# Order of waits, loads and vector work at five places of a hybrid decoder layer

## The reference

```
y_a = y_a @ w_proj_attn[layer]
y_b = o_d.reshape(b, s, D_VAL_B).astype(x.dtype) @ w_proj_delta[layer]
h = h + (gate_a * y_a + gate_b * y_b) @ w_out[layer]
hn = rmsnorm(h, norm_ffn[layer])
h = h + (jax.nn.silu(hn @ w_gate[layer]) * (hn @ w_up[layer])) @ w_down[layer]
return rmsnorm(h, norm_final)
```

## Time and profile before

| what | us |
|---|---|
| median of three runs | 2248.0 (2246.32 to 2248.94) |
| the profiled execution | 2246.41 |
| its span | 2244.7 |
| TensorE busy in it | 2187.7 |
| VectorE busy | 1119.6 |
| ScalarE busy | 917.5 |
| POOL busy | 698.9 |

### The profile page before, as it was taken

The page is one execution under the profiler, slowest core; times in us unless marked ns, Lnnn a source line. Parts: engine busy times, 40 slices in busy tenths (PEclk is TensorE's granted clock), DMA queues, the critical chain, the costliest instruction groups (busy, mean ns, idle before and its releaser), DMA issues.

```text
span 2244.7 us, 30780 instructions
## 1 busy us (share of the span) xinstructions
PE 2187.7 (97%) x11040; PEld 1823.9 (81%) x11040; DVE 1119.6 (50%) x1559; ACT 917.5 (41%) x1627; POOL 698.9 (31%) x529
## 2 busy tenths in 40 slices
PE   6999999999999999999999999999999999999998
PEld 4788787887878888888888887888788888878887
DVE  7621423314256656655665544425766666640054
ACT  5544444443345555555555632124433333320013
POOL 6885665666521111111111124321000000043340
PEclk8999999999999999999999999999999999999999
DMA  5112213123231211211211343341222222261221
GB/s 134 49 48 67 86 57 94 58 57 95 81 102 36 66 37 47 65 45 39 75 56 31 129 160 123 89 108 29 85 78 81 84 79 80 75 232 49 72 79 75
DMA packets 251922, 175.66 MB, mean 78 GB/s; under 512 B 41448, under 2 KB 225960, under 8 KB 251840
## 3 DMA queue, kind: packets, MB, share of 16 engines
q1 hardware_dynamic: 221776, 136.46, 20.7%
q10 hardware_dynamic: 30064, 38.10, 5.3%
HBM read 143.36 MB, written 31.18 MB: 78 GB/s over the span
## 4 chain that ended last, share of the span: by engine, by line
PE 85%; DVE 3%; ACT 3%; issue 3%; POOL 2%; DMA 2%; POOLq 1%; ACTq 1%; DVEq 1%; SPq 0%
PE bank L213 19%; PE bank L2273 16%; PE bank L1064 15%; PE bank L2514 10%; PE bank L1277 6%; PE bank L1527 2%; PE bank L1510 2%; PE bank L687 1%; PE bank L2289 1%; DMA raw_first<-in_w_in 1%; PE bank L1517 1%; PE bank L698 1%; PE bank L1564 1%; DVE own_sum_t L486 1%; POOL q_lo_s L941 1%
## 5 line engine op out<-in xcount | busy, mean ns | idle before, releaser
L213 PE MATMUL bank<-u_hi,w_hi 128*128 128x512 f32 x704 | 310.9, 442 | 4.2 <-ACT z_next L1749 3.0
L199 POOL CAST w_hi<-raw 128x1024 fp32r<-128x1024 f32 (+1 forms) x60 | 61.0, 1017 | 711.4 <-PE bank L213 484.7
L213 PE MATMUL bank<-u_hi,w_lo 128*128 128x512 f32 x704 | 277.0, 394 | 0.0
L213 PE MATMUL bank<-u_lo,w_hi 128*128 128x512 f32 x704 | 276.3, 392 | 0.0
L2495 POOL CAST dn_hi<-dn_raw 128x896 fp32r<-128x896 f32 (+1 forms) x24 | 31.2, 1301 | 564.9 <-DMA dn_raw<-in_w_down 460.5
L213 PEld LDWEIGHTS bank<-u_hi,w_lo 128*128 128x128 f32 x704 | 132.4, 188 | 29.0
L201 POOL TENSOR_TENSOR w_lo<-raw,w_hi 128x1024 fp32r<-128x1024 f32 (+1 forms) x60 | 151.2, 2520 | 8.6
L213 PEld LDWEIGHTS bank<-u_hi,w_hi 128*128 128x128 f32 x704 | 133.8, 190 | 20.3 <-ACT z_next L1749 3.4
L213 PEld LDWEIGHTS bank<-u_lo,w_hi 128*128 128x128 f32 x704 | 134.0, 190 | 15.0 <-issue 1.9
L941 POOL TENSOR_TENSOR q_lo_s<-q_sum_s,q_hi_s 128x512 fp32r<-128x512 f32 x92 | 122.1, 1333 | 72.8 <-ACT q_hi_s L996 67.2
L1817 DVE SCALAR_TENSOR_TENSOR conv_out<-conv_in,conv_c,conv_out 128x1024 f32<-128x1024 f32 (+1 forms) x96 | 100.3, 1045 | 15.0 <-issue 12.0
(11 more groups left out here) (433 smaller groups left out, 5864.5 us busy)
## 6 DMA issues: line engine op xcount, KB each, us to landing
raw<-in_w_in SPq DMA_DIRECT2D x36, 512.0 KB, 3.8
raw_first<-in_w_in SPq DMA_DIRECT2D x24, 512.0 KB, 3.7
raw_second<-in_w_in SPq DMA_DIRECT2D x24, 512.0 KB, 4.8
row<-scr_rows ACTq DMA_DIRECT2D x24, 512.0 KB, 4.7
raw_gate<-in_w_gate SPq DMA_DIRECT2D x22, 512.0 KB, 3.8
raw_up<-in_w_up SPq DMA_DIRECT2D x22, 512.0 KB, 3.8
scr_v<-gate_out SPq DMA_DIRECT2D x44, 256.0 KB, 2.1
tmp<-scr_gate ACTq DMA_DIRECT2D x16, 512.0 KB, 3.5
```

Of the source, the lines that this page charges most:

```text
L199: nc.gpsimd.tensor_copy(hi[:, 0:kt, :], raw[slot][:, 0:kt, :])
L213: last = nc.tensor.matmul(bank[dst][:, :], wpart[slot][wp][:, k, :], rhs[ap][:, k, half * HALF:(half + 1) * HALF], start=k == 0 and (wp, a ...
```

## The change

Five edits. In `proj_sp` the five branch loads (and the wait ahead of them) come after the load of the fifth weight tile instead of the fourth. In `merge_pe` the first group waits before each step k for the branches up to that step, in the order in which they are made, instead of for all twelve before the first. In `out_pe` the first tile runs its seven steps, the last step and the residual for both halves before the second tile begins; before, the seven steps of both tiles came first. In `up_vec` the step of a pair is divided into its additions (`up_add_vec`) and its work for the next pair (`up_next_vec`), and in the second pair of all the addition of step 4 comes ahead of the sums of step 3. In the last pair each subtraction of v comes one step later, so the first is behind the addition of step 4, and the fourth moves into `down_vec`.

```diff
@@ proj_sp
-                if f == 3:
+                if f == 4:
                     sp.wait_ge(dl["out"], NHB)
                     for t in range(NSLOT + 2, NB - 1):
                         load_branch(sp, t)
@@ merge_pe
                         if f == 0 and half == 0:
-                            pe.wait_ge(b_low, NB)
+                            pe.wait_ge(b_low, max(B_PLACE[NSLOT + kk] for kk in range(k + 1)) + 1)
@@ out_pe
                         product(0, i, half, k, (m_prod, 4 * KT - 3 + 2 * i + half))
-            pe.wait_ge(m_low, KT)
-            for i in range(2):
+                pe.wait_ge(m_low, KT)
                 for half in range(2):
                     product(0, i, half, KT - 1, None)
                     residual(0, i, half)
@@ up_step_vec, up_vec
+            up_add_vec(dve, it, b, i)
+            if not last:
+                up_next_vec(dve, it, b, i)
...
         def up_vec(dve):
-            for i in range(3, 7):
+            up_add_vec(dve, 0, 1, 4)
+            up_next_vec(dve, 0, 1, 3)
+            up_next_vec(dve, 0, 1, 4)
+            for i in range(5, 7):
                 up_step_vec(dve, 0, 1, i)
...
                     up_step_vec(dve, NFF // 2 - 1, b, i, last=b == 1)
-                    if b == 1 and i >= 3:
-                        v_low(dve, i - 3)
+                    if b == 1 and i >= 4:
+                        v_low(dve, i - 4)
@@ down_vec
-            for o in range(4, 7):
+            for o in range(3, 7):
                 v_low(dve, o)
```

More of the change, by code:

```diff
@@ L2323, in up_step_vec, with up_add_vec @@
         def up_step_vec(dve, it, b, i, last=False):
+            up_add_vec(dve, it, b, i)
+            if not last:
+                up_next_vec(dve, it, b, i)
+        def up_add_vec(dve, it, b, i):
             v = nc.vector
             p7, p3, p2 = it * 14 + 7 * b, it * 6 + 3 * b, it * 4 + 2 * b
-            q = it * 2 + (b + 1)
             first_bank, second_bank = bank[UP_BANKS[b][0]], bank[UP_BANKS[b][1]]
@@ L2349, in up_step_vec, with up_next_vec @@
                                     ALU.mult).then_inc(up["v"], 1)
-            if last:
-                return
+        def up_next_vec(dve, it, b, i):
+            q = it * 2 + (b + 1)
             if i == 2:
```

## The result

The changed kernel takes 2236.66 us (median of 5 runs, 2235.0 to 2238.16), the kernel before 2248.0: a ratio of 0.9949, 95% interval 0.9938 to 0.9960, so 11.3 us faster. Forecast were 6.7 us, to 2241.3, with a range down to 2238.0. The direction was right, the size too small, and the time lies outside the range. The profiled execution took 2236.66 us with a span of 2234.9, against 2246.41 and 2244.7: the two profiles differ by only 9.8 us. Both gaps, 6.7 to 9.8 and 9.8 to 11.3, had to be explained.

The account below looks back on a forecast made before the run. TensorE was taken as the bound, busy 2187.7 of 2244.7 us. Terms 0.57 + 2.56 + 1.19 + 1.2 + 2.9 = 8.4, less 1.7 for the clock, gave 6.7 us: 2241.3 from the median, range 2238.0 to 2245.0.

Parts of the forecast that it names:

- Weight ahead of branches: Attention projection: loading the fifth weight before the branch loads removes TensorE's wait, 0.57 us; possible loss 0 to 1.5 us.
- The 0.16 us that I added to each short idle: TensorE's short idles: first matmuls after resuming were taken as slower, costing 0.16 us beyond each idle.
- 3.13 and 3.37 in the table: Projection to first output matmul, two edits together: 3.13 us gain forecast, 3.37 us measured.
- Merge waits: Merge start: waiting branch by branch lets TensorE start without the 2.40 us idle; gain 2.56 us.
- idles near 3 us cost 1.7 us more, shorter ones do not: TensorE's idles: only those near 3 us bring the 1.2 GHz clock level behind them, losing 1.7 us.
- Output order: Output projection: closing the first tile early lets POOL start the next weight sooner; TensorE's wait goes, gain 1.19 us.
- First pair: Up projection: early addition starts TensorE 2.81 us sooner, but a new gate-half wait takes back 1.6; gain 1.2 us.
- Last pair: Up into down projection: TensorE 4.7 us early, then waits for the fourth down weight; gain 2.9, less 1.7 for the clock.
- chain of turns of VectorE and POOL: Down weights: the two engines' operations run one after the other, 10.5 us in sum, readying the fourth weight at 2004.4.
- my 90 matmuls: Down projection start: 90 matmuls, 20.4 us, have their data before TensorE needs the fourth down weight at 2000.8.
- the 1.7 us that I subtracted in vain: Down projection: the clock falls behind one 3.6 us idle, costing 1.70 us.
- The rival without slow matmuls: Down projection: no clock fall behind the new idle; gain 8.4 us, to 2239.6 us; chance 15%.

Follow-up runs that it names:

- e12: Kernel before with only the fifth projection weight loaded ahead of the five branch loads; 2247.17 us in one run.
- e2: Kernel before with only the merge's waits made branch by branch; 2244.01 us, ratio 0.9982.
- e1: Kernel before with only the last pair's edit, the addition of step 4 ahead of the first subtraction of v; 2243.43 us, ratio 0.998.
- e9: Kernel before, unedited, profiled again; 2247.95 us.
- e10: Kernel before, unedited, profiled once more; 2248.09 us.
- e11: Kernel before, unedited, third more profile; 2247.01 us.
- e8: Changed kernel with the next up weight's load issued ahead of the stores of the previous result; 2235.15 us, ratio 0.9945.
- e7: Changed kernel with the sixth and seventh subtraction of v (first chunk) replaced by ScalarE copies; 2238.32 us in one run.
- e6: Changed kernel, but the first down group waits for the third and fourth weight together before six matmuls; 2239.59 us, ratio 0.9967.
- e4: Kernel before with only the output projection's order changed, first tile ending first; 2247.86 us, ratio 0.9999.

## Why the prediction was right in direction and wrong in size

**Weight ahead of branches: right.** 0.57 us forecast, 0.7 in e12. The 0.16 us that I added to each short idle was misread, though: 2.79 is 2.40 plus a row's own 0.39 us, so 0.16 is by how much a row is longer than the distance to the next. Slower first matmuls come on top of it: behind the 0.41 us idle the distances are 0.34 us and four times 0.24, behind the 2.40 us idle one of 0.30. That makes up the 0.24 us between 3.13 and 3.37 in the table. The cover was thinner than I said, at a place that I did not look at: the sixth weight now lands behind the branches, POOL ends its split at 1343.01 + 1.29 = 1344.30, and TensorE needs it when the fifth tile, begun near 1339.0, has had its 24 matmuls, near 1344.4.

**Merge waits: mechanism right, the term too small.** The 2.56 us of the idle came (no idle in e2 and after; TensorE is at 1361.49 as the last subtraction runs). But the step "idles near 3 us cost 1.7 us more, shorter ones do not" was false. It rested on one profile. Of the eight profiles that have the 2.40 us idle, four (e1, e9, e10, e11) have the fall behind it. Of the kernel before alone it is three of four. So by my estimate about half of the executions, or more, paid 1.6 us more there, and the edit takes that away too: 0.8 us in the mean at one half, 1.2 at three quarters. The first pair's idle (1.77 to 2.70 us) had it in one of eight, 0.2 us more.

**Output order: right.** 1.19 forecast, 1.32 and 1.35 in the timelines; alone it is below what the medians can tell.

**First pair: right, with its new wait.** 1.2 forecast, 1.31 and 1.4 measured. VectorE's queue was the bound as worked out, and e8 shows what stood behind it: the transfer of the up weight, not VectorE's amount of work.

**Last pair: this step failed.** Forecast was a chain of turns of VectorE and POOL that ends at 2004.4, one idle of 3.6 us, and the 1.70 us of the low clock behind it, 1.2 us net. Measured 3.69 (e1: 3.75). The turns are real (e7), but two things were wrong. First, their end: in the frame of before it is 1997.61 + 6.03 = 2003.6, 0.8 us earlier than summed. Second, and larger, the form of the idle. I had TensorE pass the third weight and wait only for the fourth. POOL's subtraction for the third, 3.96 us beside VectorE, also came too late, by 0.88 us, and six matmuls stand between the two waits. My own chain said as much, had I asked it: its turns end the third weight at 1993.9 + 2.25 + 0.93 + 2.25 + 2.1 = 2001.4, and TensorE needs it six matmuls ahead of 2000.8, at 1999.4. The last six of my 90 matmuls did not have what they need. The idle was cut in two short ones, and the clock did not fall. e6 joins them and pays; e7 takes the first away and pays at 2.40 us. This is the 1.7 us that I subtracted in vain. The turns bind with little to spare: in the profile of after POOL begins the fourth weight at 1994.40, right behind the third with no idle, but in e7, where the turns are gone, it idles 1.82 us for that weight's transfer. The rival without slow matmuls, given 15%, was the case, and 2239.6 with it was still 3 us too high.

**The sum.** 3.37 + 1.32 + 1.31 + 3.69 = 9.7 is the difference of the two profiles. I carried the forecast from the profile's time to the median, 1.6 us higher, as if the edits could not touch that difference. They do: the profiled execution of before was one of those without the fall at the merge. Over the four profiles of before the way from the projection to the final sum is 916.81, 918.38, 917.40 and 917.77 us, mean 917.6; over the two of after 907.11 and 906.50, mean 906.8. That is 10.8 us, near the 11.3 of the medians and within their interval (9.0 to 13.9). The last half us stays open; it is below what these runs tell.

## What to carry to other kernels

An idle of TensorE above 2 us is to be priced with the low clock behind it, by its chance over several profiles, not by the one at hand; the first profile of this kernel hid a cost that four of eight profiles pay. Where an edit makes TensorE early at a bound that stays, the new idle's form matters as much as its length: two waits of 0.9 and 1.4 us with six matmuls between them were cheaper than one of 2.4. And when an engine is late by its queue, look at which transfer its first late operation waited for: moving the addition brought 1.3 of 2.8 us, and the rest came only with the load (e8).

## What the runs showed of the hardware

By idles before, and falls of the clock behind them (a stretch of 0.50 to 0.69 with matmuls of 0.63 us instead of 0.39), over the profiles that have them:

| idle of TensorE | us | with a fall |
|---|---|---|
| all others from the projection up to the final norm (many) | 0.4 to 1.77 | none |
| start of the DeltaNet phase, all profiles | 2.95 to 3.00 | 13 of 14 |
| a second idle there, e10 alone | 2.38 | 1 of 1 |
| start of the merge | 2.40 | 4 of 8 |
| last product of the first edited pair, in before and e1, e4, e9 to e12 | 2.13 to 2.70 | 1 of 7 |
| last product of the last pair | 2.23 to 3.05 | 7 of 8 |
| down weights, in one piece (e6, e7, e12) | 2.40, 2.91, 4.16 | 3 of 3 |

The shortest of these idles with a fall was 2.23 us and the longest without one 2.96, both in e10. In the final norm, where TensorE has little left to do, the clock also fell in after and e12, about 2 us behind an idle of 1.08, and no time was lost by it (10.7 us from there to the end, as in every profile). The same 2.40 us at the same instruction fell in four executions and not in four others, so length alone does not decide between these two; what does stays open. The fall did not come at one fixed moment either: from the projection on, the low level began between 0.7 us ahead of the resumption (e12, at the down weights) and 1.5 us behind it (e2, in the last pair). The price was 1.6 us at the merge, 1.7 at the last product, and more in e12.

VectorE's subtractions and POOL's operations run in turns: beside VectorE 3.96 us, without 2.13 (e7), for the same POOL subtraction. The rows of after show the turns one by one: VectorE's subtraction ends at 1992.49, 2.15 us behind the end of POOL's cast (1990.34) and about its 2.25 alone, though it had begun at 1989.47; POOL's ends at 1994.44, 1.95 us behind that, though it had begun at 1990.48. This agrees with the exclusive lock of the Trainium skill, "SBUF — State Buffer", "Who interferes with whom".
